# Turning q of the FOX attention on VectorE in 32x32 blocks instead of on TensorE

## The chip, the cores and the metric

The kernel is one launch on one core of a Trainium2 chip. The time is that of the device in microseconds (us), the median of several runs: 2745.2 us for the kernel before (3 runs, 2744.93 to 2745.22). One more execution, taken with the hardware profiler, gives the profile and the trace.

## The reference

Two blocks run one after the other on 256 tokens of width 2048, all in fp32. The first is a hybrid layer (sparse attention, gated delta rule, MLP). The second has a FOX layer (attention with a forget gate, 16 heads of 128) and a retention layer. The change touches the FOX layer alone:

```python
proj = einsum('bsd,de->bse', x, w_in)
q, k, v, gate, f_logit = split(proj, ...)
q = rms_norm_2(heads(q), q_gain)          # over the 128 of each head
k = rms_norm_2(heads(k), k_gain)
c = cumsum(log_sigmoid(f_logit + b_f))
s = einsum('bhqd,bhkd->bhqk', qb, k) * scale + c[..., :, None] - c[..., None, :]
p = softmax(where(key_pos <= q_pos, s, -inf))
o = einsum('bhqk,bhkd->bhqd', p, v)
y = einsum('bse,ed->bsd', o * silu(gate), w_out)
```

## The kernel before

All large products are cut into jobs. A job is 256 tokens x 2048 rows of a weight x 512 columns, and it has 8 granules of 256 weight rows. fp32 precision comes from splitting: each weight granule w becomes `w_hi` (ScalarE, `split_hi`, L262) and `w_lo = raw - w_hi` (VectorE, `split_lo`, L270), and TensorE makes 12 products of 128x512 per granule, 8 with `w_hi` (L295) and 4 with `w_lo` (L301). There are four buffers for the split granules. ScalarE may write the hi part of granule n+4 only when TensorE is done with granule n (semaphore `granules_done`); VectorE's lo part waits for the hi part (`hi_ready`).

The other work of a layer is woven between the granules. Each engine has a generator (`fox_mix`) that is advanced by one slot ahead of each granule: on TensorE ahead of the products of the granule, on ScalarE and VectorE ahead of the split of the granule four further on (`split_job`). So the order within an engine is written out by hand, by the count of `yield`s.

The FOX layer works through four groups of four heads. A group has four jobs, for q, k, v and gate (`f_nat[:, 0..3]`), and a generator runs over the 24 slots of three of them, from the k job on. Slots 0 to 15 matter here:

- VectorE, slots 0 to 3: square q (L2548), sum over a head (L2550) and scale (L2551), then multiply by the root (L2554) that GpSimd makes in between (L461, semaphore `f_rs_ready`), then multiply by the gain (L2556, which raises `fq_ready`). Slots 8 to 11 do the same for k. Slots 6 and 7 build the bias (L2562, L2565); slots 4, 5, 12 and 13 hold a split and nothing else.
- TensorE, slot 6: 8 transposes of q through the identity into `mx` (L1938), slot 13: 8 transposes of k; slot 14: the scores of q and k (L507, L508), from `f_T`.
- ScalarE, slots 6 and 13: two copies each of `mx` to `f_T` (L1336), then `fqk_copied`.

In `f_T`, the first four of eight blocks are q turned, the last four k turned. `block_turn` (L371) is a turn without TensorE that other stages use: a 128x128 transpose is 16 transposes of 32x32, and one VectorE instruction of shape 32x256 does a 32-row strip for all heads and both token tiles. `fox_turn` uses it for the output of a group: four instructions ahead of each of four splits.

Three groups run in a hardware loop on VectorE; the fourth (group 3) is written out. In the trace, group g spans about 95.9 us: group 1 has its scores at 1679 us, groups 0, 2 and 3 one such distance apart.

Of the kernel before, what the change touches and what calls it, by code (L numbers as in the profile page):

```python
# [21 lines left out]
ACT = mybir.ActivationFunctionType  # L22
AX = mybir.AxisListType

P = 128
S = 256
NT = S // P
# [7 lines left out]
HG = 4  # L35
# [68 lines left out]
def lin(i):  # L104
    return i if isinstance(i, Lin) else Lin(0, [(1, i)]) if not isinstance(i, int) else Lin(i)


def wait(eng, sem, n):

    n = lin(n)  # L110
    assert n.c > 0 or not n.terms, "a wait against a register that is 0 in the first round"
    if n.c > 0:
        eng.wait_ge(sem, n.value())
# [21 lines left out]
def build(nc, x, rel_table, ln1_w, w_in, pe_k, pe_v, w1_k, w2_k, w1_v, w2_v, conv_w, a_log, dt_bias,  # L135
# [4 lines left out]
    with ctx:  # L140
        def sb(name, shape, dt=F32):
            return ctx.enter_context(nc.sbuf_tensor(name, shape, dt))

        def sem(name):
            return ctx.enter_context(nc.semaphore(name))
# [11 lines left out]
        ident = sb("ident", [P, P])  # L157
# [45 lines left out]
        mx = ctx.enter_context(nc.psum_tensor("mx", [P, 4, NB], F32))  # L203
# [13 lines left out]
        def sg(name):  # L217
            if name not in S_:
                S_[name] = sem(name)
            return S_[name]  # L220
# [145 lines left out]
        def block_turn(dst, src, n0, n1):  # L366

            for n in range(n0, n1):
                i, j = n // 4, n % 4
                d = dst[32 * j:32 * j + 32].rearrange("p k (t i c) -> p t k i c", t=NT, i=4)[:, :, :, i, :]  # L370
                last = nc.vector.transpose(d, src[32 * i:32 * i + 32].rearrange(  # L371
                    "p t (k j c) -> p t k j c", j=4, c=32)[:, :, :, j, :])
            return last
# [286 lines left out]
        f_nat = at(0, 4, NT, NB)  # L660
        f_T = at(4096, 8, S)
# [48 lines left out]
        def bcast(ap, n):  # L710

            return bass.AP(tensor=ap.tensor, offset=ap.offset, ap=[*ap.ap, [0, n]])
# [241 lines left out]
        def _(act):  # L954
            A = nc.scalar.activation
# [10 lines left out]
            for r in range(GPJ):  # L966
                norm_hi(act, B_LN1 + r, LN1, lt_a, 2 * r, 1, r % 4)
                split_hi(act, 0, r, r + 1)
                if r > 3:
                    act.wait_ge(x_loaded[r - 4], 16)  # L970
                    last = block_squares(act, LN1, r - 4)
# [331 lines left out]
            with fori(2) as i:  # L1303
                g = Lin(1, [(1, i)])
# [22 lines left out]
            def fox_mix(g):  # L1327
                for kind in range(2):
                    for i in range(6 + kind):
                        if isinstance(g, int) and g == 0 and kind == 0 and i == 3:  # L1330
                            act.wait_ge(sg("f_cum_ready"), 1)
                            A(f_sums[0:FOX_HEADS, :], mx[0:FOX_HEADS, 0, 0:S], ACT.Copy).then_inc(sg("f_cum_copied"), 1)
                        yield
                    for b in range(2 * kind, 2 * kind + 2):
                        wait(act, sg("fqk_turned"), Lin(b + 1, [(4, g)]))
                        A(f_T[:, 2 * b:2 * b + 2, :], mx[:, b % 2, :].rearrange("p (c s) -> p c s", s=S),  # L1336
                          ACT.Copy).then_inc(sg("fqk_copied"), 1)
                yield
                yield from unit_act(act, Lin(4, [(1, g)]), f_sc, f_pt, 6, 2)

# [78 lines left out]
            for h in range(2):  # L1419
                for p in range(2):  # L1420
                    J = Lin(J_RET + 6 * p, [(16, h)])
                    mix = None
                    for c in range(6):
# [5 lines left out]
                        if p == 1 and c == 0:  # L1429
# [5 lines left out]
                                 lambda t, c=c: RET_QK ** -0.5 if c == 1 else 1.0, mix=mix)  # L1435
# [9 lines left out]
        def _(pe):  # L1445
            MM, TR = nc.tensor.matmul, nc.tensor.transpose
# [394 lines left out]
            for n in range(4):  # L1841

                J = J_PAB + n
                for r in range(GPJ):
# [12 lines left out]
                    for k in range(2):  # L1857
                        kt = 2 * r + k
                        for t in range(NT):
# [4 lines left out]
                            last = MM(o, a_lo, w_hi[:, r % 4, k, :], start=False, stop=(kt % 8 == 7))  # L1864
# [49 lines left out]
            def fox_mix(g):  # L1914

                one, two = Lin(1, [(1, g)]), Lin(0, [(2, g)])
                yield
                yield
                if isinstance(g, int) and g == 0:
                    pe.wait_ge(sg("f_lg_ready"), 1)  # L1920
                    MM(mx[0:FOX_HEADS, 0, 0:P], f_logf[:, 0, :], tri[:, :], start=True, stop=True)
                    MM(mx[0:FOX_HEADS, 0, P:S], f_logf[:, 0, :], f_ones[:, :], start=True, stop=False)
                    MM(mx[0:FOX_HEADS, 0, P:S], f_logf[:, 1, :], tri[:, :], start=False, stop=True) \
                        .then_inc(sg("f_cum_ready"), 1)
                for _ in range(4):
                    yield
                if isinstance(g, int) and g == 0:
                    pe.wait_ge(sg("f_cum_copied"), 1)
                wait(pe, lt_lo_ready, two + B_FO)
                for kind in range(2):  # L1930
                    wait(pe, sg("fq_ready"), two + kind + 1)
                    if kind:
                        wait(pe, sg("fqk_copied"), Lin(2, [(4, g)]))
                    for b in range(2):
                        for c in range(2):
                            for t in range(NT):
                                i = 2 * b + c
                                last = TR(mx[:, b, (2 * c + t) * P:(2 * c + t + 1) * P],  # L1938
                                          f_nat[:, kind, t, i * P:(i + 1) * P], ident[:, :])
                        last.then_inc(sg("fqk_turned"), 1)  # L1940
                    for _ in range(7 if kind == 0 else 1):
                        yield
                wait(pe, sg("fqk_copied"), Lin(4, [(4, g)]))
                yield from unit_pe(pe, Lin(4, [(1, g)]), f_sc, f_pt, lambda j: f_T[:, j, :],
                                   lambda j: f_T[:, 4 + j, :],
                                   lambda j, t: f_nat[:, 2, t, j * HD:(j + 1) * HD], 7, 2)
# [120 lines left out]
            for t in range(NT):  # L2067
                for r in range(GPJ):
# [8 lines left out]
                    for k in range(2):  # L2077
                        last = MM(o, a_hi[:, k, :], lo[:, k, :], start=False, stop=(r == GPJ - 1 and k == 1))  # L2078
# [3 lines left out]
        def _(dve):  # L2082
# [448 lines left out]
            for t in range(NT):  # L2531
                last = STT(f_t[0][:, t, :], small_ps[:, t, 0:FOX_HEADS], rstd[:, t:t + 1], bf_row, ALU.mult, ALU.add)
# [4 lines left out]
            STT(f_logf, f_t[0], 0.0, f_t[1], ALU.min, ALU.subtract).then_inc(sg("f_lg_ready"), 1)  # L2537
            def fox_mix(g, fc):
                one = Lin(1, [(1, g)])
                for kind in range(2):  # L2540
                    J = Lin(J_FOX + kind, [(4, g)])

                    wait(dve, acc_taken[J.c % 2], J.half() + 1)
                    v = f_nat[:, kind].rearrange("p t (h d) -> p (t h) d", d=HD)
                    sq = f_sc[:, :, :].rearrange("p h k -> p (h k)")[:, 0:8 * HD].rearrange(
                        "p (h d) -> p h d", d=HD)
                    ss, rs = f_ss[:, kind, :], f_rs[:, kind, :]
                    fc.link(TT(sq, v, v, ALU.mult))  # L2548
                    yield
                    fc.link(nc.vector.tensor_reduce(ss, sq, AX.X, ALU.add))  # L2550
                    TS(ss, ss, 1.0 / HD, NORM_EPS, ALU.mult, ALU.add).then_inc(sg("f_ms_ready"), 1)  # L2551
                    yield
                    wait(dve, sg("f_rs_ready"), Lin(kind + 1, [(2, g)]))
                    fc.link(TT(v, v, bcast(rs, HD), ALU.mult))  # L2554
                    yield
                    TT(v, v, heads_bcast(fgain[:, kind, :], 8), ALU.mult).then_inc(sg("fq_ready"), 1)  # L2556
                    yield
                    if kind == 0:
                        yield
                        yield  # L2560
                        wait(dve, sg("f_cum_loaded"), Lin(16, [(16, g)]))
                        STT(f_bias[:, :, 0:P], f_all[:, :, 0:P], -1.0, heads_bcast(f_causal[:, 0:P], HG),  # L2562
                            ALU.mult, ALU.add)
                        yield
                        STT(f_bias[:, :, P:SEG], f_all[:, :, :], -1.0, heads_bcast(f_causal[:, P:SEG], HG),  # L2565
                            ALU.mult, ALU.add).then_inc(sg("f_bias_ready"), 1)
                        yield
                yield
                yield
                wait(dve, sg("f_bias_ready"), one)  # L2570
                yield from unit_dve(dve, Lin(4, [(1, g)]), fc, f_sc, f_o, f_bias[:, :, :], None, True, 8)
# [66 lines left out]
            for c in range(4):  # L2638
# [7 lines left out]
                for t in range(NT):  # L2646
                    last = STT(res[:, t, cs], res[:, t, cs], ALPHA, acc[J % 2][t][:, :], ALU.mult, ALU.add)
                last.then_inc(acc_taken[J % 2], 1)
                dve.wait_ge(acc_taken[J % 2], J // 2 + 1)
                last = block_stats(c)  # L2650
# [3 lines left out]
            for c in range(D // NB):  # L2654
                cs = slice(c * NB, c * NB + NB)
                for t in range(NT):
                    last = TS(res[:, t, cs], res[:, t, cs], lnmv[:, t, 0:1], rstd[:, t:t + 1],
                              ALU.subtract, ALU.mult)
# [156 lines left out]
            for t in range(NT):  # L2815
# [6 lines left out]
                for c in range(0, D // NB, 2):  # L2822
                    for i in (c, c + 1):
                        x_ = res[:, t, i * NB:(i + 1) * NB]
                        last = STT(x_, x_, lnmv[:, t, 0:1], w_row[:, 0, i * NB:(i + 1) * NB], ALU.subtract, ALU.mult)
# [3 lines left out]
                    for i in (c, c + 1):  # L2829
                        x_ = res[:, t, i * NB:(i + 1) * NB]  # L2830
                        last = STT(x_, x_, rstd[:, t:t + 1], w_row[:, 1, i * NB:(i + 1) * NB], ALU.mult, ALU.add)
# [70 lines left out]
```

## Time and profile before

| | |
|---|---|
| median of 3 runs | 2745.2 us |
| profiled execution | 2748.31 us, span 2746.7 us |
| TensorE (PE) busy | 2703.5 us, 98% of the span |
| VectorE (DVE) busy | 1834.3 us, 67% |
| ScalarE (ACT) busy | 1282.3 us, 47% |
| GpSimd (POOL) busy | 89.4 us, 3% |
| mean granted TensorE clock | 0.994 |

The span is the stretch from the first to the last instruction. Busy shares are means over all stages. TensorE's matmuls are pipelined, so an engine shown as busy is not at its peak. In the views below L12 is line 12 of the kernel before; PEld is a weight load of TensorE; an entry in square brackets is the idle time of the engine just before the instruction, and what ended it. A row with x2 merges instructions that stand back to back.

### The profile page before, as it was taken

How to read it: one execution, taken by the hardware profiler on the slowest of the kernel's cores; microseconds unless marked ns; L12 is line 12 of the kernel's file. 1: busy time of each engine (PE TensorE's matmuls, PEld its weight loads, DVE VectorE, ACT ScalarE, POOL GpSimd, SP SyncE). 2: the span in 40 equal slices, each digit the busy share in tenths (PEclk: the TensorE clock that was granted, in tenths of full speed). 3: DMA queues.
4: the chain of work that ended last, by engine and by line, in shares of the span. 5: the costliest groups of instructions: out<-in, count | busy, mean ns of one | idle time of the engine just before them, and what ended most of it. 6: DMA issues, size and time to landing. Idle time of an engine off the chain costs nothing.

```text
span 2746.7 us, 34775 instructions
## 1 busy us (share of the span) xinstructions
PE 2703.5 (98%) x12596; PEld 2243.8 (82%) x12596; DVE 1834.3 (67%) x2388; ACT 1282.3 (47%) x1602; POOL 89.4 (3%) x105
## 2 busy tenths in 40 slices
PE   8999999999999999999999999999999999999998
PEld 7888887888788888888888888888878888888886
DVE  5555767765588567576588766765575966577766
ACT  6554645544355444344445555455353434434342
POOL 1000110100000000000000000000000000000000
PEclk9999999999999999999999999999999999999999
DMA  8754554556667666665666677686655655666663
GB/s 246 241 171 139 145 153 141 158 158 191 219 193 195 193 191 193 195 193 191 193 191 191 187 162 189 187 177 194 202 169 168 196 171 189 199 181 188 179 211 123
DMA packets 261459, 504.82 MB, mean 184 GB/s; under 512 B 16440, under 2 KB 25192, under 8 KB 260288
## 3 DMA queue, kind: packets, MB, share of 16 engines
q1 hardware_dynamic: 256448, 486.73, 59.7%
q0 software_dynamic: 4704, 16.03, 2.5%
q8 instruction: 99, 1.62, 0.2%
q14 instruction: 48, 0.39, 0.1%
q10 hardware_dynamic: 160, 0.04, 0.0%
HBM read 498.66 MB, written 4.08 MB: 183 GB/s over the span
## 4 chain that ended last, share of the span: by engine, by line
PE 94%; ACT 2%; DVE 2%; DMA 1%; issue 1%; ACTq 0%; DVEq 0%; POOL 0%
PE acc L295 55%; PE acc L301 27%; PE acc L1863 1%; PE acc L1864 1%; PE acc L1862 1%; ACT arena L535 1%; DVE w_lo L270 1%; ACT w_hi L262 1%; PE mx L508 1%; PE mx L516 0%; PE mx L341 0%; DMA res<-in_x 0%; DVE arena L2241 0%; PE acc L2078 0%; PE acc L2075 0%
## 5 line engine op out<-in xcount | busy, mean ns | idle before, releaser
L270 DVE TENSOR_TENSOR w_lo<-raw,w_hi 128x1024 fp32r<-128x1024 f32 x916 | 1121.4, 1226 | 837.3 <-ACT w_hi L262 818.6
L262 ACT ACTIVATE w_hi<-raw 128x1024 fp32r<-128x1024 f32 x916 | 968.6, 1059 | 1318.0 <-PE acc L301 1247.5
L295 PE MATMUL acc<-w_hi,lt_b_hi 128*128 128x512 f32 x1792 | 704.4, 393 | 0.0
L295 PE MATMUL acc<-w_hi,lt_b_lo 128*128 128x512 f32 x1792 | 697.6, 389 | 0.0
L295 PE MATMUL acc<-w_hi,lt_a_hi 128*128 128x512 f32 x1664 | 659.3, 396 | 0.0
L295 PE MATMUL acc<-w_hi,lt_a_lo 128*128 128x512 f32 x1664 | 651.4, 391 | 0.0
L301 PE MATMUL acc<-w_lo,lt_b_hi 128*128 128x512 f32 x1792 | 479.2, 389 | 0.0
L301 PE MATMUL acc<-w_lo,lt_a_hi 128*128 128x512 f32 x1664 | 447.1, 391 | 3.2 <-DVE w_lo L270 3.2
L295 PEld LDWEIGHTS acc<-w_hi,lt_b_hi 128*128 128x128 f32 x1792 | 336.5, 188 | 71.1 <-issue 2.1
L295 PEld LDWEIGHTS acc<-w_hi,lt_b_lo 128*128 128x128 f32 x1792 | 336.6, 188 | 70.4 <-issue 1.9
L301 PEld LDWEIGHTS acc<-w_lo,lt_b_hi 128*128 128x128 f32 x1792 | 336.4, 188 | 70.1
L301 PEld LDWEIGHTS acc<-w_lo,lt_a_hi 128*128 128x128 f32 x1664 | 314.0, 189 | 69.5 <-DVE w_lo L270 3.6
L295 PEld LDWEIGHTS acc<-w_hi,lt_a_hi 128*128 128x128 f32 x1664 | 314.4, 189 | 64.4 <-issue 0.2
L295 PEld LDWEIGHTS acc<-w_hi,lt_a_lo 128*128 128x128 f32 x1664 | 314.7, 189 | 63.2
L371 DVE STREAM_TRANSPOSE arena<-arena 32x256 f32<-32x256 f32 x464 | 202.3, 436 | 7.6
L461 POOL TENSOR_TENSOR sm<-sm 128x2 f32<-128x2 f32 (+2 forms) x20 | 24.9, 1244 | 1511.7 <-DVE sm L455 812.1
L1862 PE MATMUL acc<-w_hi,lt_b_hi 128*128 128x512 f32 x128 | 50.1, 391 | 0.0
L1864 PE MATMUL acc<-w_hi,lt_b_lo 128*128 128x512 f32 x128 | 49.9, 389 | 0.0
L1863 PE MATMUL acc<-w_lo,lt_b_hi 128*128 128x512 f32 x128 | 49.8, 389 | 0.0
L371 DVE STREAM_TRANSPOSE arena<-res 32x256 f32<-32x256 f32 x96 | 41.8, 436 | 1.6
L356 ACT ACTIVATE lt_a_hi<-arena 128x512 fp32r<-128x512 f32 x42 | 24.2, 625 | 37.3 <-DVE arena L371 37.3
L2459 DVE TENSOR_TENSOR res<-res,acc 128x512 f32<-128x512 f32 x54 | 34.5, 680 | 0.0
(396 smaller groups left out, 1544.9 us busy)
## 6 DMA issues: line engine op xcount, KB each, us to landing
raw<-in_ret_w_in SPq DMA_DIRECT2D x192, 512.0 KB, 3.8
raw<-in_w_in SPq DMA_DIRECT2D x168, 512.0 KB, 3.6
raw<-in_w_up SPq DMA_DIRECT2D x128, 512.0 KB, 3.7
raw<-in_w_down SPq DMA_DIRECT2D x128, 512.0 KB, 4.7
raw<-in_fox_w_in SPq DMA_DIRECT2D x128, 512.0 KB, 4.6
raw<-in_ret_w_out SPq DMA_DIRECT2D x64, 512.0 KB, 4.2
raw<-in_w_o SPq DMA_DIRECT2D x32, 512.0 KB, 4.5
raw<-in_fox_w_out SPq DMA_DIRECT2D x32, 512.0 KB, 4.6
```

The lines of the kernel that those rows point to most:

```text
L262: nc.scalar.activation(w_hi[:, r % 4], raw[:, slot, 2 * half:2 * half + 2, :], ACT.Copy).then_inc(hi_ready, 1)
L270: nc.vector.tensor_tensor(w_lo[:, r % 4], raw[:, slot, 2 * half:2 * half + 2, :], w_hi[:, r % 4].bitcast(F32), ALU.subtract) \
L295: nc.tensor.matmul(acc[par][t][:, :], lt[p][:, kt, t * P:(t + 1) * P], w_hi[:, r % 4, k, :], start=(kt == 0 and p == 0), stop=False)
L301: last = nc.tensor.matmul(acc[par][t][:, :], lt[0][:, kt, t * P:(t + 1) * P], w_lo[:, r % 4, k, :], start=False, stop=(kt == KT - 1))
L371: last = nc.vector.transpose(d, src[32 * i:32 * i + 32].rearrange("p t (k j c) -> p t k j c", j=4, c=32)[:, :, :, j, :])
L461: nc.gpsimd.tensor_tensor(dst, base, mhalf[:, 0:w], ALU.pow).then_inc(done, 1)
L508: last = nc.tensor.matmul(mx[:, j, P:SEG], q(j)[:, P:S], k(j), start=True, stop=True)
L535: last = nc.scalar.activation(sc[:, j, a:b], sc[:, j, a:b], ACT.Exp, bias=rowmax[:, t, j:j + 1], accum_out=esum[:, t, j:j + 1])
L1862: MM(o, a_hi, w_hi[:, r % 4, k, :], start=(kt % 8 == 0), stop=False)
L1863: MM(o, a_hi, w_lo[:, r % 4, k, :], start=False, stop=False)
L1864: last = MM(o, a_lo, w_hi[:, r % 4, k, :], start=False, stop=(kt % 8 == 7))
L2459: last = TT(res[:, t, cs], res[:, t, cs], acc[par][t][:, :], ALU.add)
```

## The change

VectorE turns q, and k stays with TensorE. The 16 block transposes stand in four slots of four: slots 4 and 5, which held a split alone, and slots 12 and 13, which also did. The last one raises `fq_ready` a third time per group. TensorE's turn of q in slot 6 and ScalarE's two copies of it go. TensorE's scores now wait for the third `fq_ready`.

```diff
 # ScalarE, fox_mix: the copies of q are gone, those of k stay in slot 13
-                    for b in range(2 * kind, 2 * kind + 2):
-                        wait(act, sg("fqk_turned"), Lin(b + 1, [(4, g)]))
-                        A(f_T[:, 2 * b:2 * b + 2, :], mx[:, b % 2, :].rearrange("p (c s) -> p c s", s=S),
-                          ACT.Copy).then_inc(sg("fqk_copied"), 1)
+                for b in range(2):
+                    wait(act, sg("fk_turned"), Lin(b + 1, [(2, g)]))
+                    A(f_T[:, HG + 2 * b:HG + 2 * b + 2, :], mx[:, b, :].rearrange("p (c s) -> p c s", s=S),
+                      ACT.Copy).then_inc(sg("fk_copied"), 1)
 # TensorE, fox_mix
-                for kind in range(2):
-                    wait(pe, sg("fq_ready"), two + kind + 1)
...
-                wait(pe, sg("fqk_copied"), Lin(4, [(4, g)]))
+                for _ in range(7):
+                    yield
+                wait(pe, sg("fq_ready"), Lin(2, [(3, g)]))
+                for b in range(2):
...
+                                      f_nat[:, 1, t, i * P:(i + 1) * P], ident[:, :])
+                    last.then_inc(sg("fk_turned"), 1)
+                yield
+                wait(pe, sg("fk_copied"), Lin(2, [(2, g)]))
+                wait(pe, sg("fq_ready"), Lin(3, [(3, g)]))
 # VectorE, fox_mix
+                def turn_q(n):
+                    return block_turn(f_T[:, 0:HG, :], f_nat[:, 0], n, n + 4)
...
                     if kind == 0:
+                        wait(dve, sg("fq_ready"), Lin(1, [(3, g)]))
+                        turn_q(0)
                         yield
+                        turn_q(4)
                         yield
...
-                yield
+                turn_q(8)
+                yield
+                turn_q(12).then_inc(sg("fq_ready"), 1)
                 yield
                 wait(dve, sg("f_bias_ready"), one)
```

On VectorE, this is what stands from the gain of k to the bias of the scores (slots 11 to 14) before; L270 is the split of one granule:

```order
L2556 TENSOR_TENSOR arena<-arena,fgain 128x1024
L113 REGISTER_ALU
L270 TENSOR_TENSOR w_lo<-raw,w_hi 128x1024 [waits hi_ready]
L113 REGISTER_ALU
L270 TENSOR_TENSOR w_lo<-raw,w_hi 128x1024 [waits hi_ready]
L113 REGISTER_ALU
L270 TENSOR_TENSOR w_lo<-raw,w_hi 128x1024 [waits hi_ready]
L113 REGISTER_ALU
L113 REGISTER_ALU [waits f_bias_ready]
L548 SCALAR_TENSOR_TENSOR arena<-mx,arena 128x1536 [waits scores_ready]
```

And the same place now, where L2559 is the gain's line:

```order
L2559 TENSOR_TENSOR arena<-arena,fgain 128x1024
L113 REGISTER_ALU
L270 TENSOR_TENSOR w_lo<-raw,w_hi 128x1024 [waits hi_ready]
L371 STREAM_TRANSPOSE arena<-arena 32x2x4x32 x4
L113 REGISTER_ALU
L270 TENSOR_TENSOR w_lo<-raw,w_hi 128x1024 [waits hi_ready]
L371 STREAM_TRANSPOSE arena<-arena 32x2x4x32 x4
L113 REGISTER_ALU
L270 TENSOR_TENSOR w_lo<-raw,w_hi 128x1024 [waits hi_ready]
L113 REGISTER_ALU
L113 REGISTER_ALU [waits f_bias_ready]
L548 SCALAR_TENSOR_TENSOR arena<-mx,arena 128x1536 [waits scores_ready]
```

Eight transposes stand in front of the splits of slots 12 and 13; the other eight stand in the same way in slots 4 and 5.

On TensorE, the scores of a group (slot 14) begin so before:

```order
L301 MATMUL acc<-w_lo,lt_b_hi 128x512 [waits lo_ready]
L301 MATMUL acc<-w_lo,lt_b_hi 128x512 x3
L507 MATMUL mx<-arena 128x128 [waits att_out_taken,fqk_copied]
L508 MATMUL mx<-arena 128x256
L507 MATMUL mx<-arena 128x128
```

And so now:

```order
L301 MATMUL acc<-w_lo,lt_b_hi 128x512 [waits lo_ready]
L301 MATMUL acc<-w_lo,lt_b_hi 128x512 x3
L507 MATMUL mx<-arena 128x128 [waits att_out_taken,fq_ready,fk_copied]
L508 MATMUL mx<-arena 128x256
L507 MATMUL mx<-arena 128x128
```

The place is the same; the wait for VectorE's last transpose is new.

## Rows read from the trace of the kernel before

**Rows 1.** The page, chain that ended last: shares of the span by engine.

```profile
PE 94%; ACT 2%; DVE 2%; DMA 1%; issue 1%; ACTq 0%; DVEq 0%; POOL 0%
```

**Rows 2.** The chain in order of time, groups 1 and 3: start us, us, what.

```profile
1654.92 0.91 PE acc L301 x4
1655.83 0.87 PE mx L1938 x8
...
1675.77 0.87 PE mx L1938 x8
...
1679.41 0.22 PE mx L507 x2
...
1867.48 0.87 PE mx L1938 x8
```

**Rows 3.** Timeline of VectorE, group 1: start us, us, instruction [idle before].

```profile
1646.32 1.21 DVE L2550 TENSOR_REDUCE arena<-arena 128x8 f32<-128x1024 f32 x1
1647.57 0.17 DVE L2551 TENSOR_SCALAR arena<-arena 128x8 f32<-128x8 f32 x1
1647.67 1.23 DVE L270 TENSOR_TENSOR w_lo<-raw,w_hi 128x1024 fp32r<-128x1024 f32 x1
1650.46 1.23 DVE L2554 TENSOR_TENSOR arena<-arena 128x1024 f32<-128x1024 f32 x1 [1.56 <-POOL arena L461]
1651.81 1.23 DVE L270 TENSOR_TENSOR w_lo<-raw,w_hi 128x1024 fp32r<-128x1024 f32 x1
1652.95 1.22 DVE L2556 TENSOR_TENSOR arena<-arena,fgain 128x1024 f32<-128x1024 f32 x1
1654.09 2.35 DVE L270 TENSOR_TENSOR w_lo<-raw,w_hi 128x1024 fp32r<-128x1024 f32 x2
...
1658.16 0.69 DVE L2562 SCALAR_TENSOR_TENSOR arena<-arena 128x512 f32<-128x512 f32 x1
```

**Rows 4.** Timeline of VectorE where `fox_turn` turns the output of group 0.

```profile
1626.09 1.78 DVE L371 STREAM_TRANSPOSE arena<-arena 32x256 f32<-32x256 f32 x4
1627.88 1.22 DVE L270 TENSOR_TENSOR w_lo<-raw,w_hi 128x1024 fp32r<-128x1024 f32 x1
1629.14 1.78 DVE L371 STREAM_TRANSPOSE arena<-arena 32x256 f32<-32x256 f32 x4
```

**Rows 5.** Timeline of GpSimd, and a split of VectorE beside it, group 1.

```profile
1647.83 2.60 POOL L461 TENSOR_TENSOR arena<-arena,sm 128x8 f32<-128x8 f32 x1 [72.75 <-DVE arena L2551]
1668.72 1.63 POOL L461 TENSOR_TENSOR arena<-arena,sm 128x8 f32<-128x8 f32 x1 [18.29 <-DVE arena L2551]
1668.79 1.23 DVE L270 TENSOR_TENSOR w_lo<-raw,w_hi 128x1024 fp32r<-128x1024 f32 x1 [0.16 <-ACT w_hi L262]
```

**Rows 6.** Timelines of VectorE (groups 0 and 3) and TensorE (groups 0 and 1).

```profile
1555.72 1.23 DVE L270 TENSOR_TENSOR w_lo<-raw,w_hi 128x1024 fp32r<-128x1024 f32 x1 [0.36 <-ACT w_hi L262]
...
1564.78 1.23 DVE L270 TENSOR_TENSOR w_lo<-raw,w_hi 128x1024 fp32r<-128x1024 f32 x1 [1.78 <-ACT w_hi L262]
...
1578.38 1.23 DVE L270 TENSOR_TENSOR w_lo<-raw,w_hi 128x1024 fp32r<-128x1024 f32 x1
...
1845.56 2.35 DVE L270 TENSOR_TENSOR w_lo<-raw,w_hi 128x1024 fp32r<-128x1024 f32 x2
...
1583.39 0.38 PE L507 MATMUL mx<-arena 128*128 128x128 f32 x2
...
1679.25 0.38 PE L507 MATMUL mx<-arena 128*128 128x128 f32 x2
```

**Rows 7.** Waits, timeline and windows (clock: third from the end) of TensorE elsewhere.

```profile
PE mx L516 <- ACT arena L535: 3.4, 3, 2.0
...
737.90 1.19 PE L301 MATMUL acc<-w_lo,lt_a_hi 128*128 128x512 f32 x4 [3.15 <-DVE w_lo L270]
...
738.00:743.00 5.00, 5.00 (x15) 3.97 (x16) 5.00 (x6) 1.06 (x1) 0.00 (x0) 0.66 0.65 198
147.00:152.00 5.00, 3.04 (x28) 2.66 (x27) 3.00 (x3) 5.00 (x12) 0.00 (x0) 1.00 0.86 309
```

More of the change, by code:

```diff
@@ L1929, in fox_mix @@
                 wait(pe, lt_lo_ready, two + B_FO)
-                for kind in range(2):
-                    wait(pe, sg("fq_ready"), two + kind + 1)
[L1932 to L1941, printed above, removed]
-                        yield
-                wait(pe, sg("fqk_copied"), Lin(4, [(4, g)]))
+                for _ in range(7):
+                    yield
+                wait(pe, sg("fq_ready"), Lin(2, [(3, g)]))
+                for b in range(2):
+                    for c in range(2):
+                        for t in range(NT):
+                            i = 2 * b + c
+                            last = TR(mx[:, b, (2 * c + t) * P:(2 * c + t + 1) * P],
+                                      f_nat[:, 1, t, i * P:(i + 1) * P], ident[:, :])
[3 more added lines that the diff above has]
+                wait(pe, sg("fq_ready"), Lin(3, [(3, g)]))
                 yield from unit_pe(pe, Lin(4, [(1, g)]), f_sc, f_pt, lambda j: f_T[:, j, :],
```

## The prediction

> **What bounds the kernel now.** I read the page first. The chain that ended last is 94% TensorE [rows 1], so time is saved where TensorE issues less and lost where it stands still; work on other engines costs only if TensorE comes to wait for it. Then the chain in order of time through one FOX group: TensorE goes from granule to granule without a gap, 8 transposes of q take 0.87 us of it (1655.83), the 8 of k another 0.87 (1675.77), and the scores follow at 1679.41 [rows 2]. Last, the timeline of VectorE beside it: in the FOX stage it has gaps that end on ScalarE's hi part, which itself waits for TensorE (the brackets of [rows 6]). The reader should see two things. VectorE has time to spare over a group. But from the end of q's normalization to the scores there is a fixed number of slots, and the question is whether VectorE's whole chain of work still fits into these.
>
> Starts in the chain stand 0.16 us after those in the timeline (1679.41 against 1679.25 for the same scores [rows 2, 6]); below I compare timeline with timeline.
>
> **What is removed.** Per group 8 transposes of q on TensorE, 0.87 us in the chain, and 0.02 for a refilled pipe: 0.89 us, four groups 3.6 us. ScalarE's two copies go as well; ScalarE waits for TensorE at that point and has nothing to give back, so they count as zero. The lo part of a granule is needed only four granules after its slot, so a VectorE that is 3 us late does not stop the large products by itself. If TensorE never waited, the result would be -3.6 us.
>
> **What is added.** 16 transposes per group on VectorE, four in each of four slots. The same instruction, in the same shape, with a split between, is in the trace: four of them start 1.79 us before the next split, and the split starts 1.26 us before the next transposes [rows 4]. Behind other instructions a split takes 1.14 us from start to start (1651.81 to 1652.95 [rows 3]). So a slot with a turn is 3.05 us, against a granule of TensorE of 12 products at 0.91 / 4 us = 2.73 us [rows 2]. Each turn slot makes VectorE 0.3 us later, and there was a lateness to begin with: in groups 1 to 3 VectorE comes out of the previous group's turn with its splits back to back (x2 at 1654.09 [rows 3]).
>
> **The chain for group 1,** from the split at 1654.09 [rows 3], start to start, every step from a row: 1.14 to the first turn (1655.23); 1.79 + 1.26 + 1.79 to the split of slot 5 (1660.07); 1.14 to the first bias; 0.60 for it (its 0.69 less 0.09, the overlap of 1651.81 + 1.23 with 1652.95) to a split (1661.81); 1.14 to the second bias and 1.14 behind it, a full 128x1024 instruction, to the split of slot 7 (1664.09); 1.14 to the square of k and 1.35, as behind L2554 (1650.46 to 1651.81), to a split (1666.58); 1.14 to the sum and 1.25 to its scaling L2551 (1668.97). Here GpSimd makes the root and VectorE waits.
>
> How long it waits has two values in the trace. Where VectorE's split started before GpSimd's instruction (1647.67 against 1647.83), this one took 2.60 us; where the split came after it (1668.79 against 1668.72), 1.63 us [rows 3, 5]. In group 1 before the change k had the short one, because the split was waiting for ScalarE. With VectorE late the hi part lies ready, the split follows 0.10 us behind L2551 (1647.57 to 1647.67), and the long one applies: 2.89 us from L2551 to L2554 (1647.57 to 1650.46). That gives 1671.86.
>
> The Trainium skill, page "SBUF — State Buffer", section "SBUF: two separate sides", says that VectorE with two SBUF inputs and GpSimd share a port pair under an exclusive lock, and the later one waits for the whole instruction of the other. By that rule the long value holds whenever VectorE runs back to back; the 2.60 against 1.63 of this trace agree. Without it the sum would be 0.97 us less in each of groups 1 to 3.
>
> On: 1.35 to a split (1673.21), 1.14 to the gain of k (1674.35, done 1675.57). TensorE reaches k's transposes at 1675.77 - 0.89 = 1674.88 and waits 0.7 us, which by itself would not matter, since q is later still: 1.14 to a split (1675.49), 1.26 to the third turn (1676.75), 1.79 and 1.26 to the fourth (1679.80), 1.78 to its end, 1681.58. For waking and refilling TensorE I add 0.17: four products behind a wait took 1.19 us [rows 7], against 3 x 0.23 + 0.39 = 1.07 in a row, and 0.05 for the semaphore, an estimate. The scores start in effect at 1681.75, before at 1679.25 [rows 6]. **Group 1 loses 2.5 us,** the saved 0.89 already in it: TensorE stands about 2.4 us at the scores.
>
> I see nothing behind it that gives this back. Queued on TensorE behind the scores are the granules; the bias of the scores, the exponentials and the next splits all start from what TensorE has finished and move with it.
>
> **The other groups.** Group 2 stands as group 1: 2.5. Group 3 starts its split at 1845.56, where 1654.09 plus the distance of the groups (1867.48 - 1675.77 = 191.71) would be 1845.80, so it is 0.24 ahead: 2.3. Group 0 has no turn before it. Its split is at 1555.72, after waiting for ScalarE; the turns bring the split of slot 6 to 1555.72 + 1.14 + 1.79 + 1.26 + 1.79 + 1.14 + 0.60 = 1563.44, and the hi part comes at 1564.78 - 0.89 = 1563.89 [rows 6]: back in step, GpSimd short. From the split 1578.38 - 0.89 = 1577.49 then 1.26 + 1.79 + 1.26 + 1.78 + 0.17 = 6.26 gives 1583.75, before 1583.39: 0.4 us lost.
>
> **Sum:** 0.4 + 2.5 + 2.5 + 2.3 = 7.7 us. On the profiled execution the span goes from 2746.7 to 2754.4 and its time from 2748.3 to 2756.0. The median of the runs is 3.1 us under the profiled time; on it the forecast is 2745.2 + 7.7 = **2752.9 us**. Bounds of the two steps that no row shows: the turn into `f_T` could take between what the row has and 10% more (four turns, +0.7 us a group), and the waking between 0 and 0.4 us; the unknown lies within about 2 us of the total.
>
> **Rivals.**
>
> 1. *The clock falls.* TensorE stood 3.15 us at 737.90 and its granted clock was 0.66 over the next 5 us: it ran in part at 1.2 instead of 2.4 GHz, which lost (1 - 0.66) x 5 = 1.7 us. A wait of 2.0 us (L516) left it at 1.00 [rows 7]. Mine is 2.4, nearer to the second. If it falls in one to three of the groups: 2754.6 to 2758.0 us. The Trainium skill, page "TensorE: Matmul & The Clock Gate", section "Why this matters for your kernels", warns of idle gaps between bursts of matmuls; it would speak for this rival if the wait came out longer. Chance 0.13.
> 2. *GpSimd is quick in spite of it:* 1.63 us everywhere. Then groups 1 to 3 lose 0.97 less each, 2.9 in all: 2749.9 us. Against it: the two values go with who came first. Chance 0.12.
> 3. *VectorE catches up* between slots 6 and 11 in all groups, as in group 0, so that only slots 12 and 13 count: 4 x 0.4 = 1.6, 2746.8 us, not slower by what can be measured. It decides from the point where the split of slot 9 in group 1 again waits for ScalarE: the hi part is there at 1668.79 - 0.89 = 1667.90 [rows 5], and by my chain the split starts at 1669.07, 1.2 us after it. Chance 0.09.
> 4. *q is in time:* -3.6 us, 2741.6 us, not even then a gain that can be told. It needs a fourth turn that ends 3.3 us earlier than my chain has it. Chance 0.04.
>
> Forecast 0.62.
>
> **How the numbers follow.** A measurement of this kernel tells about 0.2%, 5.5 us, from no change, that is 2739.7 to 2750.7. My case lies 2.2 us over that edge; of its 0.62 about 0.06 falls under it. Slower: 0.56 + 0.13 + 0.02 of rival 2 = 0.71. Same: 0.06 + 0.10 + 0.09 + 0.02 = 0.27. Faster: 0.02. The range reaches from rival 3 to three falls of the clock: 2746.5 to 2758.0 us.
>
> **What would show it.** In the trace of the changed kernel: the 8 transposes of slot 6 gone; at the scores of groups 1 to 3 a wait of TensorE for VectorE's transposes of 2.1 to 2.7 us, in group 0 of about 1; a wait at k's transposes of 0.7 us; GpSimd's root for k at 2.6 us in groups 1 to 3 and 1.6 in group 0; distances between the groups about 2.5 us longer. I am wrong if the waits at the scores are under 1.5 us in groups 1 to 3, or if time goes at a place outside slots 4 to 14.

## The result and the profile after

The change makes the kernel slower, by 0.3 to 0.4%. Four runs of the changed kernel gave 2753.36, 2759.84, 2758.36 and 2759.24 us (median 2758.8), beside 2745.21 us for the kernel before; the ratio was 1.0042, 95% interval 1.0030 to 1.0054. Six more in a second set gave 2756.35 us, where 25 runs of the kernel before gave 2747.59 us: ratio 1.0032 (1.0019 to 1.0045), 8.8 us. The forecast was +7.7 us.

The time of a whole run scatters more than I had assumed: the 25 runs of before lie between 2741.3 and 2753.5 us. So the traces are compared over one stretch that holds the whole FOX attention, from the first product of the forget gate to the first transpose of the normalized residual on TensorE. These are its two ends in the trace of before (timeline of TensorE; start us, us, instruction, [idle before]):

```profile
1548.02 0.39 PE L1921 MATMUL mx<-arena 128*16 128x128 f32 x2
...
1998.49 4.39 PE L1979 MATMUL mx<-ident,res 128*128 128x128 f32 x20 [5.25 <-DVE res L2657]
```

And after, where lines have moved:

```profile
1544.08 0.39 PE L1921 MATMUL mx<-arena 128*16 128x128 f32 x2
...
2003.55 0.66 PE L1978 MATMUL mx<-ident,res 128*128 128x128 f32 x2 [5.25 <-DVE res L2665]
```

450.5 us before, 459.5 after: +9.0. The stage began 3.9 us earlier after than before, from causes ahead of the changed place (what moves such starts is in the last section), so the span grew by 5.0 only, from 2746.7 to 2751.7. The page's chain now reads so, against [rows 1]:

```profile
PE 83%; issue 11%; DVE 2%; ACT 2%; DMA 1%; POOL 0%; ACTq 0%; DVEq 0%; POOLq 0%
```

The "issue" share is no cost by itself: TensorE is busy for 2700.1 us, 3.4 less than before, so it did not stand still for 11% of the span; the chain could not be followed through some stretches of the FOX stage. The waits of TensorE from 1540 to 2000 us say what happened (who waited for whom, us in total, times, longest):

```profile
PE mx L507 <- issue: 7.7, 4, 2.2
PE mx L1937 <- DVE arena L2559: 1.6, 3, 0.7
```

Neither wait is in the trace of before. L507 is the first product of the scores. Its releaser is shown as "issue"; that it is VectorE's last transpose is seen from the two timelines. VectorE in group 1, after (compare [rows 3]):

```profile
1650.53 1.22 DVE L270 TENSOR_TENSOR w_lo<-raw,w_hi 128x1024 fp32r<-128x1024 f32 x1
1651.66 1.77 DVE L371 STREAM_TRANSPOSE arena<-arena 32x256 f32<-32x256 f32 x4
...
1665.39 0.17 DVE L2554 TENSOR_SCALAR arena<-arena 128x8 f32<-128x8 f32 x1
1665.49 1.23 DVE L270 TENSOR_TENSOR w_lo<-raw,w_hi 128x1024 fp32r<-128x1024 f32 x1
1668.24 1.23 DVE L2557 TENSOR_TENSOR arena<-arena 128x1024 f32<-128x1024 f32 x1 [1.53 <-POOL arena L461]
...
1670.73 1.22 DVE L2559 TENSOR_TENSOR arena<-arena,fgain 128x1024 f32<-128x1024 f32 x1
1671.87 1.22 DVE L270 TENSOR_TENSOR w_lo<-raw,w_hi 128x1024 fp32r<-128x1024 f32 x1
1673.12 1.78 DVE L371 STREAM_TRANSPOSE arena<-arena 32x256 f32<-32x256 f32 x4
1674.91 1.23 DVE L270 TENSOR_TENSOR w_lo<-raw,w_hi 128x1024 fp32r<-128x1024 f32 x1
1676.17 1.79 DVE L371 STREAM_TRANSPOSE arena<-arena 32x256 f32<-32x256 f32 x4
```

TensorE's scores in groups 0 to 3, after (compare the L507 rows of [rows 6]):

```profile
1579.74 0.46 PE L507 MATMUL mx<-arena 128*128 128x128 f32 x2 [1.06 <-issue]
...
1678.07 0.46 PE L507 MATMUL mx<-arena 128*128 128x128 f32 x2 [2.20 <-issue]
...
1776.38 0.46 PE L507 MATMUL mx<-arena 128*128 128x128 f32 x2 [2.20 <-issue]
...
1874.24 0.46 PE L507 MATMUL mx<-arena 128*128 128x128 f32 x2 [2.20 <-issue]
```

The last transpose of group 1 ends at 1676.17 + 1.79 = 1677.96, and the scores start at 1678.07. In group 1 VectorE does not wait anywhere from the gain of q on except at GpSimd's root (1.53), and that root took its long time in groups 1 to 3 (GpSimd, k of groups 0 and 1, compare [rows 5]):

```profile
1568.03 1.66 POOL L461 TENSOR_TENSOR arena<-arena,sm 128x8 f32<-128x8 f32 x1 [15.88 <-DVE arena L2554]
...
1665.65 2.56 POOL L461 TENSOR_TENSOR arena<-arena,sm 128x8 f32<-128x8 f32 x1 [18.78 <-DVE arena L2554]
```

In group 2 it was long before the change too. There the hi part of the split behind L2551 lay ready already, so the split started first (1764.69), GpSimd after it:

```profile
1764.85 2.56 POOL L461 TENSOR_TENSOR arena<-arena,sm 128x8 f32<-128x8 f32 x1 [18.57 <-DVE arena L2551]
```

So the change made k's root long in groups 1 and 3 only.

One more thing shows in group 3. The chain in order of time there:

```profile
1872.04 2.20 issue
1874.24 0.46 PE mx L507 x2
1874.70 0.63 PE mx L508 x2
1875.33 0.43 PE mx L507 x2
1875.76 0.85 PE mx L508 x2
```

Two products L508 take 0.43 us undisturbed; here 0.85. The granted clock was down. Windows behind the waits of groups 1, 2 and 3 (clock: third from the end):

```profile
1676.00:1681.00 5.00, 2.93 (x18) 2.72 (x19) 3.16 (x7) 1.02 (x1) 0.00 (x0) 1.00 0.77 225
1774.00:1779.00 5.00, 2.80 (x18) 2.47 (x17) 3.43 (x6) 1.06 (x1) 0.00 (x0) 1.00 0.75 195
1876.00:1881.00 5.00, 5.00 (x21) 4.25 (x20) 1.76 (x1) 0.00 (x0) 0.00 (x0) 0.78 0.32 105
```

TensorE ran for part of the last one at 1.2 instead of 2.4 GHz. In all 13 traces, windows of 20 us from 1540 to 1980 us show the granted clock below 1.00 only at the scores behind such waits.

### The profile page after: what moved, and what is told of

It reads as the page before. It is cut to its first block, busy times and chain, and to the rows that moved or that the text cites. A ratio compares the mean times of both kernels' runs of the same rounds, so it can differ in the third digit from the quotient of the medians.

```text
span 2751.7 us, 34766 instructions
## 1 busy us (share of the span) xinstructions
PE 2700.1 (98%) x12564; PEld 2238.8 (81%) x12564; DVE 1861.1 (68%) x2452; ACT 1278.5 (46%) x1594; POOL 89.2 (3%) x105
## 4 chain that ended last, share of the span: by engine, by line
PE 83%; issue 11%; DVE 2%; ACT 2%; DMA 1%; POOL 0%; ACTq 0%; DVEq 0%; POOLq 0%
PE acc L295 48%; PE acc L301 24%; PE acc L1862 1%; PE acc L1864 1%; PE acc L1863 1%; DVE w_lo L270 1%; ACT w_hi L262 1%; ACT arena L535 0%; PE mx L341 0%; POOL arena L461 0%; PE mx L508 0%; DMA res<-in_x 0%; DVE arena L2240 0%; PE acc L2077 0%; PE mx L516 0%
## 5 line engine op out<-in xcount | busy, mean ns | idle before, releaser
L270 DVE TENSOR_TENSOR w_lo<-raw,w_hi 128x1024 fp32r<-128x1024 f32 x916 | 1121.6, 1226 | 805.2 <-ACT w_hi L262 787.3
L301 PE MATMUL acc<-w_lo,lt_b_hi 128*128 128x512 f32 x1792 | 479.0, 389 | 0.0
L301 PE MATMUL acc<-w_lo,lt_a_hi 128*128 128x512 f32 x1664 | 446.7, 390 | 2.1 <-DVE w_lo L270 2.1
L301 PEld LDWEIGHTS acc<-w_lo,lt_b_hi 128*128 128x128 f32 x1792 | 336.4, 188 | 70.1
L301 PEld LDWEIGHTS acc<-w_lo,lt_a_hi 128*128 128x128 f32 x1664 | 313.5, 188 | 68.4 <-DVE w_lo L270 2.5
L371 DVE STREAM_TRANSPOSE arena<-arena 32x256 f32<-32x256 f32 x528 | 229.9, 435 | 8.6
```

What stands on the lines that cost most here:

```text
L270: nc.vector.tensor_tensor(w_lo[:, r % 4], raw[:, slot, 2 * half:2 * half + 2, :], w_hi[:, r % 4].bitcast(F32), ALU.subtract) \
L301: last = nc.tensor.matmul(acc[par][t][:, :], lt[0][:, kt, t * P:(t + 1) * P], w_lo[:, r % 4, k, :], start=False, stop=(kt == KT - 1))
```

## The experiments

The measure is the stretch described above, from one trace each. The times of the runs stand beside it; they scatter by 2 to 3 us (standard deviation) in every kernel that was run six times or more. Where an expectation was given as a distance from before, the sum stands in the table.

| kernel | stretch, us | expected | median time (runs) | before beside it |
|---|---|---|---|---|
| before | 450.5 | | | |
| changed | 459.5 | | 2758.8 (4) | 2745.2 (4) |
| changed, again | 459.5 | | 2756.35 (6) | 2747.6 (25) |
| TensorE busy in the wait | 458.2 | 458.5 | 2755.3 (6) | 2747.6 (25) |
| scores of k | 449.1 | 449.0 | 2744.1 (12) | 2747.6 (25) |
| scores one slot later | 447.9 | 449.0 | 2745.8 (12) | 2747.6 (25) |
| before, with VectorE's turns | 450.4 | 450.5 to 451.0 | 2748.3 (10) | 2748.3 (23) |
| no turn at all | 446.8 | 446.9 | 2739.6 (1) | 2748.3 (23) |
| bias late | 452.2 | 451.9 | 2749.2 (10) | 2748.3 (23) |
| bias late, scores later | 445.6 | 445.9 | 2740.4 (7) | 2748.3 (23) |
| wait for the root first | 463.0 | 459.5 | 2762.9 (1) | 2745.0 (1) |
| changed, two more profiles | 461.1, 459.5 | 457.8 to 461.2 | 2753.2, 2755.3 (1 each) | 2745.0 (1) |

**The changed kernel once more.**

> The changed kernel once more, timed in more rounds. Theory (waits and clock): TensorE stands about 1.1 us at the scores of group 0 and 2.2 us at those of groups 1 to 3, which with the shorter TensorE work is +7.3 us against the kernel before; on top comes 1.7 us for each group in which the granted clock falls after the wait, which differs from run to run. So the runs lie between 2752.5 (no fall) and 2759 (three or four falls), in steps of about 1.7 us. Rival (another cost, always there): the first time of 2753.4 was an outlier and all runs lie together within 1 us of 2759.

Measured: 2754.1 to 2759.6 us in six runs, with the same waits in the trace as at first (7.7 us at L507, 1.7 at L1937) and again one fall of the clock, in group 3. The runs are neither all at 2759 nor in clear steps. The rival falls, but the falls of the clock alone do not make the spread either: the kernel before, without these waits, spreads as much.

**TensorE kept busy in the wait.**

```diff
                 wait(pe, sg("fk_copied"), Lin(2, [(2, g)]))
+                for n in range(16):
+                    TR(mx[:, 2 + n // 8, (n % 4) * P:(n % 4 + 1) * P],
+                       f_nat[:, 1, n % 2, (n // 4) * P:(n // 4 + 1) * P], ident[:, :])
                 wait(pe, sg("fq_ready"), Lin(3, [(3, g)]))
```

> As the changed kernel, but TensorE repeats 16 transposes of k into two unused banks in front of its wait for q (about 1.75 us of work that nobody needs). Theory (waits and clock): the work lies inside the wait of 2.2 us, the scores start when they did, and the clock no longer falls in groups 1 to 3; group 0, where the wait was 1.06 us, gets 0.7 us longer. So +7.3 + 0.7 = +8 us, 2753.2 us, with a spread between runs under 1 us and the clock at 1.00 from 1550 to 1900 us. Rival (the excess over 7.3 us has nothing to do with the clock): 13 us and more over before, 2759 us, or later still by the added work.

Its TensorE at the scores of group 1:

```profile
1674.39 1.09 PE L1937 MATMUL mx<-ident,arena 128*128 128x128 f32 x8 [0.69 <-DVE arena L2562]
...
1678.08 1.91 PE L1943 MATMUL mx<-ident,arena 128*128 128x128 f32 x16
1680.40 0.49 PE L507 MATMUL mx<-arena 128*128 128x128 f32 x2 [0.41 <-DVE arena L371]
```

The releaser now has its name: the transposes of VectorE. The added work fills the wait up to 0.4 us. The clock stays up in all groups, and the stretch is 458.2 us, +7.8 where +8 was expected. This is one trace: behind the empty wait the clock fell 5 times in 12 (below), and three groups without a fall could then be chance. That the added work keeps the clock up is not shown. The time is 7.7 us over before beside it (2755.3 against 2747.6), as expected. Between the changed kernels, 2755.3 us against 2756.35 with the empty wait, the 1 us is not clear of the scatter, and the spread of 6 us in place of under 1 us refutes that part of the expectation.

**The scores of k in place of q.**

```diff
-                wait(pe, sg("fq_ready"), Lin(3, [(3, g)]))
-                yield from unit_pe(pe, Lin(4, [(1, g)]), f_sc, f_pt, lambda j: f_T[:, j, :],
+                yield from unit_pe(pe, Lin(4, [(1, g)]), f_sc, f_pt, lambda j: f_T[:, 4 + j, :],
```

> As the changed kernel, but the scores take k in place of q (the output is thus not the reference's), so TensorE does not wait for the turn of q; VectorE still makes all 16 transposes a group. Theory (the wait at the scores is the cost): only the saved transposes of TensorE and the waits at k's turn (about 0.7 us in three groups) are left: -3.6 + 2.1 = -1.5 us, 2743.7 us, no fall of the clock. Rival (VectorE's load costs by itself, through late splits or through GpSimd): still over 2748 us.

The stretch is 449.1 us: -1.4 where -1.5 was expected. The one wait of TensorE in it:

```profile
PE mx L1937 <- DVE arena L2558: 1.6, 3, 0.7
```

With VectorE doing all its work, the stretch is 10.4 us shorter than in the changed kernel (459.5 - 449.1) once the wait for q is gone: 1.7 of it the one fall of the clock (priced below at 1.64), 8.7 the waits at the scores (7.7) and the refilling behind them. The load without the wait at the scores is not the main cost. The median, 2744.1 us, is 3.5 us below before beside it (ratio 0.9991, 0.9982 to 1.0000).

**The scores one slot later.**

```diff
 # ScalarE, TensorE and VectorE, each ahead of the scores' part of fox_mix
                 yield
+                yield
```

> As the changed kernel, but the scores and all that follows them in a group stand one slot later on TensorE, ScalarE and VectorE. Theory (the slot is the trouble, not the work): TensorE has one more granule, 2.7 us, before it needs q, and does not wait there; what is left is the 0.7 us at k's turn in three groups: 2743.7 us as with the scores of k. Rival (the time is given back): the end of the attention now meets the gate product and the next group's first slots, and TensorE or the next group's k waits there: 2746 us or more.

TensorE's waits at the scores are gone, the stretch is 447.9 us, 1.2 less than with the scores of k. The rival falls in the trace: nothing is given back. The median of 2745.8 us would not have decided it, with 2747.6 for before beside it (ratio 0.9991, 0.9982 to 0.9999). Most of the 1.2 lies between the first score and the first transpose of the probabilities (L516), 1698.32 - 1682.08 = 16.24 us in group 1, against 1695.73 - 1679.25 = 16.48 before, four times 0.24:

```profile
1682.08 0.38 PE L507 MATMUL mx<-arena 128*128 128x128 f32 x2
...
1698.32 0.38 PE L516 MATMUL mx<-ident,arena 128*128 128x128 f32 x2
```

ScalarE copies the finished job (L985) ahead of the exponentials (L535) in the old order, and in the trace of before the last exponential of group 1 ends at 1695.09 + 0.49 = 1695.58, 0.15 us ahead of L516. One slot later a split stands between the two, and the last exponential ends at 1696.76 + 0.50 = 1697.26, 1.06 us ahead of L516.

**VectorE's turns added to the kernel before.**

```diff
+                def turn_q(n):
+                    return block_turn(f_oT, f_nat[:, 0], n, n + 4)
...
+                        wait(dve, sg("fq_ready"), Lin(1, [(2, g)]))
+                        turn_q(0)
                         yield
+                        turn_q(4)
                         yield
...
+                turn_q(8)
                 yield
+                turn_q(12)
                 yield
```

> The kernel before, with VectorE's 16 transposes of q added in the same four slots, into a buffer that nobody reads; TensorE still turns q and waits for nothing new. The stretch from the first forget-gate product to the turn of the normed residual was 450.5 us in the trace of before, 459.4 to 459.5 in those of the changed kernel. Theory (the load is free, the wait is what costs): k's gain ends 0.1 us ahead of TensorE at most, so the stretch stays at 450.5 to 451.0 us. Rival (VectorE's 28 us of transposes cost by themselves): 453 us or more.

450.4 us, and a ratio of 0.9997 (0.9987 to 1.0006). 28 us more of VectorE's work cost nothing while TensorE turns q itself. The gain of k ends at 1666.07 + 1.22 = 1667.29, 0.1 us ahead of TensorE:

```profile
1666.07 1.22 DVE L2560 TENSOR_TENSOR arena<-arena,fgain 128x1024 f32<-128x1024 f32 x1
```

```profile
1667.39 1.05 PE L1938 MATMUL mx<-ident,arena 128*128 128x128 f32 x8
```

So the wait at k's turn in the changed kernel comes about because TensorE, without its own turn of q, is 0.9 us earlier at it.

**No turn of q at all** (the kernel with the scores of k, without the four `turn_q`).

> As the kernel with the scores of k, and VectorE makes no transposes of q either (the output is not the reference's). Both theories: TensorE's 32 transposes alone are gone, 446.9 us for the same stretch (3.6 us under before), no wait at k's turn and GpSimd's root for k at 1.6 us again in at least two of groups 1 to 3. If the waits at k's turn stay, VectorE was not late through the turns.

446.8 us, and GpSimd's root for k in group 1 is short again, as in groups 2 and 3:

```profile
1661.58 1.63 POOL L461 TENSOR_TENSOR arena<-arena,sm 128x8 f32<-128x8 f32 x1 [17.40 <-DVE arena L2553]
```

This is the full worth of TensorE's 32 transposes: 3.7 us. With the scores of k it was -1.4; the 2.3 between are the waits at k's turn (1.6) and what follows from them, which thus come from the transposes on VectorE.

**The bias late.**

```diff
                         turn_q(4)
                         yield
-                        wait(dve, sg("f_cum_loaded"), Lin(16, [(16, g)]))
-                        STT(f_bias[:, :, 0:P], ...)
                         yield
-                        STT(f_bias[:, :, P:SEG], ...).then_inc(sg("f_bias_ready"), 1)
                         yield
...
                 turn_q(12).then_inc(sg("fq_ready"), 1)
                 yield
+                wait(dve, sg("f_cum_loaded"), Lin(16, [(16, g)]))
+                STT(f_bias[:, :, 0:P], ...)
+                STT(f_bias[:, :, P:SEG], ...).then_inc(sg("f_bias_ready"), 1)
                 wait(dve, sg("f_bias_ready"), one)
```

> As the changed kernel, but the two instructions that build the bias (1.7 us) move on VectorE from slots 6 and 7 to slot 14, behind the turns and ahead of the bias of the scores, when VectorE waits for the scores anyway. Theory (the lateness carried from slots 4 and 5 is what makes the waits 2.2 instead of 1.1 us): VectorE is back in step at slot 7, GpSimd's root for k takes 1.6 us, the wait at k's turn goes, and the wait at the scores is 1.1 us in all groups: 450.5 + 4 x 0.35 = 451.9 us for the stretch. Rival (only where the last turn stands matters, or the late bias delays the exponentials): 455 us or more.

VectorE in group 1:

```profile
1662.20 1.23 DVE L270 TENSOR_TENSOR w_lo<-raw,w_hi 128x1024 fp32r<-128x1024 f32 x1 [0.34 <-ACT w_hi L262]
...
1664.92 1.23 DVE L270 TENSOR_TENSOR w_lo<-raw,w_hi 128x1024 fp32r<-128x1024 f32 x1 [0.16 <-ACT w_hi L262]
1666.51 1.23 DVE L2557 TENSOR_TENSOR arena<-arena 128x1024 f32<-128x1024 f32 x1 [0.36 <-POOL arena L461]
```

It waits for ScalarE again in slots 8 and 9, that is, it is back in step; the root is quick (the wait for it is 0.36 instead of 1.53). The only waits of TensorE left in the stretch:

```profile
PE mx L507 <- issue: 4.4, 4, 1.3
```

Stretch 452.2 us, expected 451.9. The clock stayed up. The time agrees, 2749.2 us against 2748.3 (ratio 1.0008, 0.9997 to 1.0019). What VectorE carried over from slots 4 and 5 was worth 5.6 us at equal clock (457.8, which is 459.5 less one fall of the clock, - 452.2), half of the 11.0 that the changed kernel loses against no turn at all (457.8 - 446.8).

**Both.**

> The bias late and the scores one slot later, together. Theory: no wait at k's turn, none at the scores, and none of the 0.5 us at the turn of the probabilities, as in the kernel with the later scores: 450.5 - 3.6 - 1.0 = 445.9 us for the stretch, and about 4.6 us less than before in the time, 2743 us where before has 2747.6. Rival (the bias of the scores, now behind the bias, makes the exponentials late by about 1 us per group): 450 us for the stretch.

445.6 us, no wait of TensorE anywhere in the attention, and a median of 2740.4 us against 2748.3: ratio 0.9969 (0.9958 to 0.9980). This is faster than the kernel before, by 0.3%, and than the changed one, with q turned on VectorE. It is 1.2 us below the kernel without any turn of q (446.8), as the later scores alone were 1.2 below the scores of k. The 7.9 us of the medians (5.5 to 11.5 by the interval) are more than the 4.8 of the stretch; where the other 3 come from no run shows.

**The wait for the root ahead of the split.**

```diff
                     TS(ss, ss, 1.0 / HD, NORM_EPS, ALU.mult, ALU.add).then_inc(sg("f_ms_ready"), 1)
+                    if kind == 1:
+                        wait(dve, sg("f_rs_ready"), Lin(2, [(2, g)]))
                     yield
```

> As the changed kernel, but for k VectorE waits for GpSimd's root right behind L2551 (the scaling), ahead of the split of slot 9 instead of behind it. Theory (who comes first gets the port pair, the other waits): GpSimd's root for k takes 1.6 us in all groups although VectorE is late in groups 1 to 3, where it took 2.56 us; from the scaling to the multiplication it is then 1.9 + 1.1 = 3.0 us or a little more, as long as before, so the stretch stays at 459.5 us with one fall of the clock and 457.8 without. Rival (GpSimd is slow there for another reason): 2.5 us again, and the multiplication about 1 us later, 3 us on the stretch.

GpSimd in group 1, the roots of q (untouched) and k:

```profile
1652.91 2.60 POOL L461 TENSOR_TENSOR arena<-arena,sm 128x8 f32<-128x8 f32 x1 [76.73 <-DVE arena L2554]
1674.28 1.63 POOL L461 TENSOR_TENSOR arena<-arena,sm 128x8 f32<-128x8 f32 x1 [18.77 <-DVE arena L2554]
```

With VectorE's split behind it, k's root takes 1.63 us in groups 1 to 3, late or not, and 1.66 in group 0: the long time comes from the split that starts first. The opposite case, a split that is held because GpSimd started first, is not in these traces: the split at 1668.79 [rows 5] started 0.07 us after GpSimd and took its usual 1.23. The stretch is 463.0, not 459.5: that part was wrong. I had left out two things: group 0, which was in step, loses 1.0 us (its wait at the scores is 2.09 in place of 1.06), and k's gain comes 0.3 us later in the others. And the clock fell twice, in groups 0 and 3. 457.8 + 1.0 + 0.9 + 2 x 1.64 = 463.0.

**Two more profiles of the changed kernel.**

> The changed kernel, one more profile, to see in how many groups the clock falls behind the wait of 2.2 us. If the fall depends on when the wait comes and not on its length alone, one or two of three groups, with 1.7 us each on the stretch: 459.5 to 461.2 us. If one of the three always: 459.5 us and in group 3 again.

The clock fell in groups 1 and 2, and not in group 3:

```profile
1676.00:1681.00 5.00, 5.00 (x20) 4.30 (x20) 1.86 (x2) 0.00 (x0) 0.00 (x0) 0.66 0.61 186
1776.00:1781.00 5.00, 5.00 (x20) 4.26 (x20) 1.59 (x2) 0.00 (x0) 0.00 (x0) 0.66 0.86 177
1876.00:1881.00 5.00, 5.00 (x27) 4.30 (x26) 2.25 (x2) 0.00 (x0) 0.00 (x0) 1.00 0.47 150
```

The stretch is 461.1 us, where 461.2 was expected for two.

> The same once more: 459.5 us for one fall of the clock, 457.8 for none, 461.2 for two.

459.5 us, one fall, in group 3.

In the four traces of the changed kernel the same wait of 2.20 us occurred twelve times and the clock fell behind five. A fall costs 1.64 us: from the scores to L516 it is 18.22 us in group 1 of the trace with two falls (1694.03 - 1675.81), 16.58 where the clock stays. With the kernel that waits for the root first, whose waits were 2.09 to 2.21 us and whose clock fell behind two of four, it is 7 of 16. Behind the waits of 1.0 to 1.3 us (the four of the kernel with the late bias, and group 0 of the changed one in four traces) it fell in none of eight.

## Why the prediction was right, and where it was not

**The chain on VectorE** was right to the tenth. From the split of slot 3 to the end of the last transpose it was to take 1681.58 - 1654.09 = 27.49 us; it took 1677.96 - 1650.53 = 27.43. Single steps agree as well: 14.86 us to the scaling L2554 (forecast 14.88), 22.59 to the third turn (22.66). The 0.17 us for waking and refilling rested on an estimate of 0.05 for the semaphore, which no row shows; measured were 0.11 from the last transpose to the scores (1677.96 to 1678.07) and 0.08 more for the first two products (0.46 against 0.38). A sum of starts from rows of the same instructions held here because VectorE ran without gaps. Two sums of the prediction are off without moving it: 3 x 0.23 + 0.39 is 1.08, not 1.07, and rival 2 comes to 2750.0, not 2749.9.

**GpSimd's root** was long in groups 1 to 3 and short in group 0, as derived from who comes first, and putting it first made it short. The rival that it stays quick is refuted for the changed kernel. The Trainium skill's rule of a lock on the shared ports ("SBUF — State Buffer", section "SBUF: two separate sides") agrees with 2.56 against 1.63 us where VectorE is first; that the lock holds VectorE too when GpSimd is first, no run here shows.

**The waits:** forecast about 2.4 us at the scores of groups 1 to 3 and about 1 in group 0, 0.7 at k's turn; measured 2.20, 1.06 and 0.70, 0.69, 0.26. **Group by group**, from the distances of the L507 rows (95.86, 95.85, 95.85 before; 98.33, 98.31, 97.86 after): 2.47, 2.46 and 2.01 where I had 2.5, 2.5 and 2.3; and group 0 from the start of the stretch, 35.66 - 35.37 = 0.3 where I had 0.4. In group 3 the split behind L2554 of the kernel before starts 1.26 us after it (1862.16 to 1863.42), not 1.35, which I had not taken over; after the change the split behind the square of k does so too (1858.03 to 1859.29). Sum without the clock 7.3 us, forecast 7.7.

**Nothing given back,** and the large products were never short of a lo part: right, TensorE has no other new wait.

**The gain of 3.6 us** that the change aims at is real (3.7 us with no turn at all) and was lost to the new wait: 11.0 us of waiting and refilling against it. VectorE's 28 us of work are free while TensorE turns q too; without its turns TensorE comes 0.9 us earlier to that of k, and there they cost 2.3 us in all.

**The clock was the step I sized wrong.** I gave 0.13 to its falling behind the new waits, because 2.4 us lay nearer to the undisturbed wait of 2.0 than to the 3.15 that had brought it down [rows 7]. It fell in every one of the four traces, 1.25 times on average, 2.1 us in the mean. The likelier case was mine plus one fall. Forecast 7.7 us, stretch 9.0 to 10.7, time 8.8 in the larger set of runs. That 7.7 lies so near to 8.8 is in part luck: the 0.4 us too much at full clock made up for part of the 2.1 too little for the clock. Two points on an axis, 2.0 and 3.15, did not bear a threshold between them; the same wait of 2.20 us did both. What in the timing of a wait decides is open.

**The first median,** 2758.8 us, lies 0.8 us above my range, though 1.0042 times 2745.2 is 2756.7. The 13.6 us between the first medians did not come back (8.8 in the next set). A further cost in the stretch is ruled out for the trace of the first run (2753.4 us), which has the same 459.5 us there as two later ones. For the three slower runs there is no trace; the scatter of whole runs is the likely reason.

**The rival "VectorE catches up"** decided nothing as the kernel stands, but its condition was the right one: with 1.7 us of work taken out of slots 6 and 7, VectorE came back in step in slot 8, and the loss went to 1.7 us.

## What to carry to other kernels

Work moved to an engine with free time is free only if its result is not awaited at a fixed slot: add up, start to start, everything that stands on that engine between its input and the slot where the result is needed. Then move other work out of that stretch or the consumer back; here one slot later and two instructions moved turned +7.3 us at full clock into -4.8. A wait of TensorE of about 2 us has a second price, a clock that may fall (here behind 7 of 16 waits of 2.1 to 2.2 us, 1.64 us each), and it must be counted as a chance.

## What the runs showed of the hardware that I had not expected

The whole time depends on the granted clock in places that no one touched. The 25 and 23 runs of the kernel before have a standard deviation of 2.8 and 3.3 us, and their time goes with the mean granted clock of the run (correlation -0.87 and -0.95, 2.4 and 2.9 us per 0.001). The stretches from 165 to 235 and 735 to 750 us, in the traces of before and of the kernel with the added turns, whose code is the same there:

```profile
165.00:235.00 70.00, 65.45 (x341) 54.67 (x340) 31.54 (x57) 33.39 (x65) 0.00 (x0) 0.90 0.44 128
735.00:750.00 15.00, 12.10 (x46) 9.84 (x47) 9.41 (x9) 4.19 (x4) 0.00 (x0) 0.89 0.72 246
```

```profile
165.00:235.00 70.00, 65.42 (x361) 55.23 (x360) 33.82 (x60) 35.61 (x68) 0.00 (x0) 0.98 0.47 135
735.00:750.00 15.00, 15.00 (x68) 12.43 (x67) 12.13 (x17) 6.37 (x6) 0.00 (x0) 1.00 0.81 272
```

At most (1 - 0.90) x 70 = 7.0 us are lost to the clock in the first and 1.4 in the second; at most, because TensorE also stands still in this time. Then there is the idle time ahead of L301, 3.15 us at 737.90 in the trace of before [rows 7] and 0.84 in the other:

```profile
731.31 1.20 PE L301 MATMUL acc<-w_lo,lt_a_hi 128*128 128x512 f32 x4 [0.84 <-DVE w_lo L270]
```

The same instructions put the sum together. The wait at L1604 ends at 170.66 us in before and at 170.41 in the other (0.3 apart); the wait at L301 begins at 734.75 and 730.47 (4.3 apart) and ends at 737.90 and 731.31 (6.6 apart); the FOX stretch begins at 1548.02 and 1539.81 (8.2 apart). So all of the 8.2 us by which the spans differ (2746.7 and 2738.5) lie ahead of the stretch: 4.0 where the clock differs between 165 and 235 us, 2.3 in the longer wait, and 1.6 behind it, where only before has the low clock. What makes the clock fall in one execution and not in the next is open. A change of 0.2% in this kernel is read from its own stretch of the trace, not from the run.
